# Depthwise convolution of both channel tiles on TensorE: four taps of 32 channels in one contraction, over shifted copies made by on-chip transfers

## The reference, cut to what matters

```python
def conv_module(a, gate, w_dw, b_dw, ln_g, ln_b, w_pw):
    u = a * jax.nn.sigmoid(gate)                     # 272 tokens x 256 channels
    y = lax.conv_general_dilated(u, w_dw[:, None, :], window_strides=(1,),
                                 padding=[(CONV_WIDTH - 1, 0)],      # 31 taps, causal
                                 dimension_numbers=('NWC', 'WIO', 'NWC'),
                                 feature_group_count=D_CONV) + b_dw  # one filter per channel
    y = jax.nn.silu(layer_norm(y, ln_g, ln_b))
    return y @ w_pw
```

## Time and profile before

| | |
|---|---|
| runs of the kernel before, median (lowest to highest of 3) | 1790.46 us (1790.15 to 1790.73) |
| the profiled execution, device time | 1793.75 us |
| its span (first to last instruction) | 1791.9 us |
| PE, DVE, ACT, POOL busy | 96%, 65%, 46%, 13% |
| granted TensorE clock, mean over the span | 0.979 |
| bytes moved | 281.5 MB, mean 157 GB/s |

### The profile page before, as it was taken

The page is one execution under the profiler, slowest core; times in us unless marked ns, Lnnn a source line. Parts: engine busy times, 40 slices in busy tenths (PEclk is TensorE's granted clock), DMA queues, the critical chain, the costliest instruction groups (busy, mean ns, idle before and its releaser), DMA issues.

```text
span 1791.9 us, 32601 instructions
## 1 busy us (share of the span) xinstructions
PE 1713.9 (96%) x13384; PEld 1662.4 (93%) x13384; DVE 1172.3 (65%) x1594; ACT 817.4 (46%) x1062; POOL 237.6 (13%) x212
## 2 busy tenths in 40 slices
PE   7999999999999999999999996999899999889998
PEld 6999999899999999998899995998899998889997
DVE  5556597685566755587686544566866568677664
ACT  5333373563435433364564433564533345354333
POOL 0002400310032000500230042231100020020000
PEclk9999999999999999999999998998999999999998
DMA  5545443344544445442355552332445533144552
GB/s 208 170 181 185 167 150 118 118 165 167 196 172 150 176 172 204 148 174 97 127 194 188 204 194 95 115 133 95 165 177 192 194 141 106 50 143 184 187 204 78
DMA packets 37864, 281.52 MB, mean 157 GB/s; under 512 B 4384, under 2 KB 4512, under 8 KB 7184
## 3 DMA queue, kind: packets, MB, share of 16 engines
q1 hardware_dynamic: 36016, 271.73, 42.3%
q0 software_dynamic: 1760, 8.56, 1.4%
HBM read 279.23 MB, written 1.05 MB: 156 GB/s over the span
## 4 chain that ended last, share of the span: by engine, by line
PE 76%; DVE 10%; ACT 7%; issue 3%; DMA 2%; POOL 1%; SPq 0%; ACTq 0%; DVEq 0%; POOLq 0%
PE bank L682 24%; PE bank L684 23%; PE bank L683 23%; DVE w_lo L2045 4%; ACT w_hi L1422 4%; DMA raw<-in_up_w 1%; ACT h L1486 1%; ACT h_hi L1485 1%; PE bank L1035 1%; POOL h L618 1%; PE bank L1060 0%; PE bank L987 0%; PE bank L703 0%; PE bank L1220 0%; DVE h L2212 0%
## 5 line engine op out<-in xcount | busy, mean ns | idle before, releaser
L2045 DVE TENSOR_TENSOR w_lo<-raw,w_hi 128x2048 fp32r<-128x2048 f32 (+3 forms) x239 | 580.6, 2429 | 277.8 <-ACT w_hi L1422 277.5
L682 PE MATMUL bank<-h_hi,w_hi 128*128 128x272 f32 (+1 forms) x2336 | 673.4, 288 | 21.2 <-DVE h_lo L2201 10.0
L684 PE MATMUL bank<-h_hi,w_lo 128*128 128x272 f32 (+1 forms) x2336 | 669.4, 287 | 0.0
L683 PE MATMUL bank<-h_lo,w_hi 128*128 128x272 f32 (+1 forms) x2336 | 668.1, 286 | 0.0
L1422 ACT ACTIVATE w_hi<-raw 128x2048 fp32r<-128x2048 f32 (+2 forms) x242 | 481.5, 1990 | 316.5 <-PE bank L684 311.7
L682 PEld LDWEIGHTS bank<-h_hi,w_hi 128*128 128x128 f32 x2336 | 444.3, 190 | 27.9 <-issue 16.3
L684 PEld LDWEIGHTS bank<-h_hi,w_lo 128*128 128x128 f32 x2336 | 444.3, 190 | 0.0
L683 PEld LDWEIGHTS bank<-h_lo,w_hi 128*128 128x128 f32 x2336 | 443.5, 190 | 0.1
L682 PE MATMUL bank<-g_hi,w_hi 128*128 128x256 f32 (+1 forms) x1344 | 386.8, 288 | 13.8 <-DVE y L2253 4.0
L684 PE MATMUL bank<-g_hi,w_lo 128*128 128x256 f32 (+1 forms) x1344 | 382.6, 285 | 0.0
L683 PE MATMUL bank<-g_lo,w_hi 128*128 128x256 f32 (+1 forms) x1344 | 381.7, 284 | 0.0
(11 more groups left out here) (363 smaller groups left out, 1863.3 us busy)
## 6 DMA issues: line engine op xcount, KB each, us to landing
raw<-in_up_w SPq DMA_DIRECT2D x131, 1024.0 KB, 4.8
raw<-in_down_w SPq DMA_DIRECT2D x48, 1408.0 KB, 5.9
raw<-in_in_w SPq DMA_DIRECT2D x20, 1024.0 KB, 4.9
raw<-in_out_w SPq DMA_DIRECT2D x16, 1024.0 KB, 4.9
raw<-in_even_w SPq DMA_DIRECT2D x12, 1024.0 KB, 4.9
raw<-in_odd_w SPq DMA_DIRECT2D x6, 1024.0 KB, 4.8
diag<-in_conv_w POOLq DMA_DIRECT2D x4, 1024.0 KB, 5.1
raw<-in_in_w SPq DMA_DIRECT2D x4, 512.0 KB, 3.5
```

The lines of the kernel that those rows point to most:

```text
L682: pe.matmul(out, w[0], x[0], start=first, stop=False)
L683: pe.matmul(out, w[0], x[1], start=False, stop=False)
L684: return pe.matmul(out, w[1], x[0], start=False, stop=last)
L2045: last = dve.tensor_tensor(lo[:, b:n], raw[:, slot, b:n], hi[:, b:n].bitcast(F32), ALU.subtract)
```

## The change

Both channel tiles go to PE. Four taps are put into one contraction: the 128 rows of the stationary operand are 4 taps x 32 channels, its 32 columns are the same 32 channels, and the moving operand holds in its four groups of 32 partitions the same 32 channels shifted by 0, 1, 2 and 3 tokens. So 31 taps are 8 steps (`TAP_STEPS`), and there are 4 groups of 32 channels in each of 2 channel tiles: 64 matmuls with 272 moving columns, each into 32 partitions of bank 4 or 5. The four groups of a step follow one another. The shifted copies `u4` are made from `upad` by 16 transfers, each of 32 partitions x 2 x 300 floats, which SP issues after the load of chunk 6, having waited for `conv_in`. `upad` gets two more zero columns, and `diag`, of the same 1 MB, comes in one transfer. The matmuls all stand after chunk 6 (ahead of the pool mixing). The vector taps go, and the wait for `conv_done` moves ahead of the scores, since these use bank 4 too. ACT adds the bias of both tiles in chunk 7's place.

The diff, less the placing of `u4` in memory and the host's laying out of the gains:

```diff
@@ -40,7 +40,10 @@
 RMS_EPS = 1e-6
 HEADS = 4
 TAPS = 31
-TAP_HALF = 16
+TAP_ROWS = 4
+TAP_STEPS = -(-TAPS // TAP_ROWS)
+TAP_COLS = P // TAP_ROWS
+U4 = T + TAP_ROWS * (TAP_STEPS - 1)
 KTOK = [(0, 128), (128, 128), (256, 16)]
 SEEN_FROM = [max(0, 64 * ((lo - META) // 64) + META) for lo, _ in KTOK]
 SEEN_AT = [0, T, 2 * T - SEEN_FROM[1]]
@@ -52,7 +55,7 @@
 IN_GROUPS = [2] * 10 + [1] * 2
 OUT_CHUNKS = KD // 2
 EVEN_GROUPS = [2] * 12 + [1]
-CONV_AT = (5, 7)
+CONV_AT = 6
 ODD_GROUPS = [2] * 6
 
 
...
@@ -204,12 +207,15 @@
+        u4 = place("u4", [P, 2, TAP_ROWS, U4], offset=u4_at)
-        upad = one("upad", [P, 2, TAPS - 1 + T])
+        upad = one("upad", [P, 2, U4 + TAP_ROWS])
@@ -232,8 +238,8 @@
-        diag = place("diag", [P, TAP_HALF, P], offset=sq_at)
-        few = placer(region((sq_at + TAP_HALF * P * 4, sq_at + KD * T4)))
+        diag = place("diag", [P, 2, TAP_ROWS, TAP_STEPS, TAP_COLS], offset=sq_at)
+        few = placer(region((sq_at + 2 * TAP_STEPS * P * 4, sq_at + KD * T4)))
@@ -373,7 +379,7 @@
         small_done = sem("small_done")
         conv_in = sem("conv_in")
         diag_loaded = sem("diag_loaded")
-        diag_used = sem("diag_used")
+        taps_loaded = sem("taps_loaded")
         conv_mm = sem("conv_mm")
         conv_done = sem("conv_done")
         conv_mean = sem("conv_mean")
@@ -561,14 +567,25 @@
                             load(src[bass.ds(c * 2 + i * n + j, 1)].rearrange("a p n -> (a p) n"), blocks, j, c)
                     st.c += n
 
-            def straight(chunks):
+            def straight(chunks, then=lambda i: None):
                 for i, (src, blocks) in enumerate(chunks):
                     load(src, blocks, i)
+                    then(i)
                 st.c += len(chunks)
+
+            def shifted_taps(l):
+
+
+                sp.wait_ge(conv_in, l + 1)
+                for r in range(TAP_ROWS):
+                    for g in range(TAP_ROWS):
+                        sp.dma_start(u4[TAP_COLS * r:TAP_COLS * (r + 1), :, g, :],
+                                     upad[TAP_COLS * g:TAP_COLS * (g + 1), :, r:r + U4]).then_inc(taps_loaded, 16)
 
             for l in range(LAYERS):
                 ffn(l * 2)
-                straight([(a["in_w"][l, c, :, 0:n * KD * P], n * KD) for c, n in enumerate(IN_GROUPS)])
+                straight([(a["in_w"][l, c, :, 0:n * KD * P], n * KD) for c, n in enumerate(IN_GROUPS)],
+                         lambda c: shifted_taps(l) if c == CONV_AT else None)
                 straight([(a["out_w"][l, c], 2 * KD) for c in range(OUT_CHUNKS)])
                 ffn(l * 2 + 1)
             straight([(a["even_w"][c, :, 0:n * KD * P], n * KD) for c, n in enumerate(EVEN_GROUPS)])
@@ -637,9 +654,7 @@
                     .then_inc(mixw_loaded, 16)
 
                 pool.wait_ge(conv_in, seen.next(conv_in))
-                pool.dma_start(diag[:], a["conv_w"][l, 0]).then_inc(diag_loaded, 16)
-                pool.wait_ge(diag_used, l + 1)
-                pool.dma_start(diag[:], a["conv_w"][l, 1]).then_inc(diag_loaded, 16)
+                pool.dma_start(diag[:], a["conv_w"][l]).then_inc(diag_loaded, 16)
                 if l == LAYERS - 1:
                     first.lo = META
                 residual_sums(2)
@@ -991,18 +1006,18 @@
             for l in range(LAYERS):
                 ffn(T, DEFER if l else 0, l == 0)
 
-                def conv_taps(c):
-
-
-                    for part in range(2):
-                        if c != CONV_AT[part]:
-                            continue
-                        pe.wait_ge(conv_in, l + 1)
-                        pe.wait_ge(diag_loaded, (2 * l + part + 1) * 16)
-                        for i in range(part * TAP_HALF, min((part + 1) * TAP_HALF, TAPS)):
-                            last = pe.matmul(ps[5][:, 0:T], diag[:, i % TAP_HALF, :], upad[:, 1, i:i + T],
-                                             start=i == 0, stop=i == TAPS - 1)
-                        last.then_inc(conv_mm if part else diag_used, 1)
+                def conv_taps():
+
+
+                    pe.wait_ge(diag_loaded, (l + 1) * 16)
+                    pe.wait_ge(taps_loaded, (l + 1) * 16 * TAP_ROWS ** 2)
+                    for j in range(2):
+                        for i in range(TAP_STEPS):
+                            for g in range(TAP_ROWS):
+                                last = pe.matmul(ps[4 + j][TAP_COLS * g:TAP_COLS * (g + 1), 0:T], diag[:, j, g, i, :],
+                                                 u4[:, j, g, TAP_ROWS * i:TAP_ROWS * i + T],
+                                                 start=i == 0, stop=i == TAP_STEPS - 1)
+                        last.then_inc(conv_mm, 1)
 
                 def score(hd):
 
@@ -1065,7 +1080,8 @@
                 def mixers(c):
 
 
-                    conv_taps(c)
+                    if c == CONV_AT:
+                        conv_taps()
                     if c == 6:
                         pe.wait_ge(mixw_loaded, seen.next(mixw_loaded, 16))
                         pe.wait_ge(pool_in, seen.next(pool_in))
@@ -1076,10 +1092,10 @@
                     elif c == 7:
                         pe.wait_ge(rope_ready, seen.next(rope_ready, 2 * HEADS))
                         pe.wait_ge(small_done, seen.next(small_done, 2))
+                        pe.wait_ge(conv_done, seen.next(conv_done, 2))
                         score(0)
                         score(1)
                         score_tails()
-                        pe.wait_ge(conv_done, seen.next(conv_done, 2))
                         for j in range(2):
                             last = pe.matmul(ps[5][:, 0:T], ones[:], conv_y[:, j, :], start=j == 0, stop=j == 1)
                         last.then_inc(conv_mean, 1)
@@ -1766,14 +1782,15 @@
 
 
                     if c == 7:
+                        for j in range(2):
+                            act.wait_ge(conv_mm, seen.next(conv_mm))
+                            act.activation(conv_y[:, j, :], ps[4 + j][:, 0:T], ACT.Identity, bias=vcol(l, V_CDB + j))\
+                                .then_inc(conv_done, 1)
                         act.wait_ge(pool_mixed, seen.next(pool_mixed))
                         for j in range(2):
                             act.activation(y[:, j, :], ps[6 + j][:, 0:T], ACT.Identity, scale=vcol(l, V_PSC + j))\
                                 .then_inc(small_done, 1)
                     elif c == 8:
-                        act.wait_ge(conv_mm, l + 1)
-                        act.activation(conv_y[:, 1, :], ps[5][:, 0:T], ACT.Identity, bias=vcol(l, V_CDB + 1))\
-                            .then_inc(conv_done, 1)
                         for j in range(2):
                             act.wait_ge(conv_cent, seen.next(conv_cent))
                             act.activation(conv_sq[:, j, :], conv_y[:, j, :], ACT.Square).then_inc(conv_sqd, 1)
@@ -2449,6 +2466,7 @@
 
                 ffn(IN_GROUPS[0] * KD, T, l, 0, l > 0)
                 dve.memset(xpad[:, :, 0:16], 0.0)
+                dve.memset(upad[:, :, TAPS - 1 + T:], 0.0)
                 link(dve.memset(upad[:, :, 0:TAPS - 1], 0.0))
 
                 def pool_windows():
@@ -2466,22 +2484,6 @@
                     link(last)
                     dve.tensor_tensor(pool_y[:], pool_y[:], xpad[:, :, 16:W], ALU.subtract).then_inc(pool_in, 1)
 
-                def conv_tap(i):
-
-                    u, w = upad[:, 0, i:i + T], vcol(l, V_DW + i)
-                    out = acc[:] if i % 2 else conv_y[:, 0, :]
-                    if i == 0:
-                        ins = dve.tensor_scalar(out, u, w, vcol(l, V_CDB), ALU.mult, ALU.add)
-                    elif i == 1:
-                        ins = dve.tensor_scalar(out, u, w, None, ALU.mult)
-                    else:
-                        ins = dve.scalar_tensor_tensor(out, u, w, out, ALU.mult, ALU.add)
-                    ins.then_inc(dve_seq, 1)
-                    seen.skip(dve_seq, 1)
-                    dve.wait_ge(dve_seq, seen.at(dve_seq, 0 if i == TAPS - 1 else -1))
-                    if i == TAPS - 1:
-                        dve.tensor_tensor(conv_y[:, 0, :], conv_y[:, 0, :], acc[:], ALU.add).then_inc(conv_done, 1)
-
                 def rope(i):
 
                     dst = (qT if i < HEADS else kT)[:, i % HEADS, :]
@@ -2499,7 +2501,7 @@
                 renormalise(take)
                 take(2)
                 dve.wait_ge(z_copied, seen.at(z_copied, 4))
-                dve.tensor_tensor(upad[:, :, TAPS - 1:], ca[:], cg[:], ALU.mult).then_inc(conv_in, 1)
+                dve.tensor_tensor(upad[:, :, TAPS - 1:TAPS - 1 + T], ca[:], cg[:], ALU.mult).then_inc(conv_in, 1)
                 split_next(2 * KD, 0, 5)
                 dve.wait_ge(conv_in, seen.next(conv_in))
                 seen.skip(q_ready, DEFER)
@@ -2565,8 +2567,7 @@
                     dve.tensor_tensor(y[:, 4 + hd, :], y[:, 4 + hd, :], ps[SCALE_BANKS[hd]][:, 0:T], ALU.mult)\
                         .then_inc(ret_done, 1)
 
```

(23 more changed lines are left out.)

## The result

The changed kernel takes 1800.51 us (median of 7 runs, 1796.03 to 1801.96); the kernel before, run beside it, 1790.73 (7 runs, 1790.15 to 1795.13). The ratio is 1.0040, 95% interval 1.0026 to 1.0054: slower by 4.7 to 9.7 us. The forecast was 3.3 us more with a range of 1790 to 1809: the sign and the range hold, the size was too small, and 3.3 lies outside both intervals.

A forecast was written before the change was run, and what follows sets the result against it. TensorE, busy 96% of the span, was taken to bound the kernel. Per layer -0.83 - 0.33 + 2.1 + 0.7 = +1.6, twice +3.3 us, on 1790.46 gave 1793.8 us, range 1790 to 1809.

The forecast's parts named there:

- the main case: Whole kernel: 3.3 us slower, 1793.8 us, by itself 1791.7 to 1795.8; chance 0.67.
- taps in pairs: Taps after chunk 6: only two column groups run at once, 14.5 us per layer; total +17.8, 1808; chance 0.14.
- taps fed too slowly: Taps after chunk 6: groups overlap but 128 records take 9.9 us; total +8, 1798.5; chance 0.07.
- Term 1a: Before chunk 6: without two vector taps ahead of it, `w_lo` comes earlier, -0.83 us per layer.
- 1b: At the mean matmul: PE's wait on `conv_y` goes, -0.33 us per layer.
- chunk 6 starts before 268.0: Layer 0, PE's start of chunk 6: forecast at 268.07; earlier than 268.0 would show the forecast wrong.
- Term 2: Chunk 6: PE idles 7.5 us before it, so granted clock falls to 0.50 behind; +2.1 us per layer (1.35 to 2.7).
- Term 3: Taps after chunk 6: 64 matmuls four at a time take 7.6 us against 6.88; +0.7 us per layer (0.4 to 1.1).
- Term 4: The 16 shifted copies on SP's queue: issues take 5.3 us, chunk 7's load goes out at about 257; cost 0.
- Term 5: Other edits: ACT's two `conv_y` copies in chunk 7's place, one more DVE memset, order after chunk 7; cost 0.
- everything after chunk 8 as before: Profile after chunk 8: expected unchanged, only 1.6 us later per layer.

The follow-up runs named there:

- the run with fewer vector taps: Kernel before, with 28 of the 31 VectorE taps of channel tile 0 left out, so half of the convolution is not computed: 1789.88 us, ratio 0.9983.
- the version with the taps in the hole and 8 fillers: Changed kernel, its 64 taps moved behind chunk 5 with 8 unused f32 matmuls ahead of them: 1784.08 us, ratio 0.9949 to the kernel before.
- the last filled one: Changed kernel, taps behind chunk 5, six copies issued by ScalarE, 4 and 10 unused matmuls ahead of the taps in layers 0 and 1: 1785.42 us, ratio 0.9960.
- the one with GpSimd: Changed kernel, taps behind chunk 5, eight of the 16 copies issued by GpSimd's queue: 1786.17 us, ratio 0.9965 to the kernel before.

## Why the prediction was right in sign and short in size

By luck the range holds: the main case alone had 1791.7 to 1795.8, and 1800.51 lies within 1790 to 1809 only because this was widened for taps in pairs and for taps fed too slowly, and neither is what happened.

The trace lets each step be read by itself. From the start of chunk 5 to that of chunk 8 layer 0 is 1.31 us longer than before and layer 1 2.24.

- **Term 1a, 1b (-0.83, -0.33): right.** Chunk 6 starts 13.76 us after chunk 5 (253.90 to 267.66) instead of 14.66 (254.24 to 268.90), 0.90 less, and the wait before the mean is gone. The run with fewer vector taps gives 0.88 and 0.40 alone. That chunk 6 starts before 268.0 was named as a sign of being wrong; it starts at 267.66, but this execution was 0.34 us ahead of the one before already at chunk 5.
- **Term 2 (+2.1, 1.35 to 2.7): right in kind, too small.** Chunk 6 lost 1.97 and 2.87 us in the changed kernel's first profile, 2.42 and 2.41 in the second: 2.4 in the mean. I had averaged five stalls of 3 to 4 us; the hole here is 7.4 us, and layer 1 had 6.23 us at 0.50 behind it, longer than any of the five. Whether the longer hole is the reason isn't shown, since behind the same hole layer 0 had 4.23.
- **Term 3 (+0.7): right.** 7.47 us for 6.88, +0.59. Nothing is seen of the 0.1 us at either end. Four column groups reading different data overlap as fully as the narrow tiles of the earlier trace rows; the rivals of pairs (14.5 us) and of weak feeding (9.9) fall. The 9.2 us worked out from the Trainium skill (TensorE: Matmul & The Clock Gate, Measured speedup vs the span model) fall with them: this trace doesn't agree with that share. 29.0 / 7.47 is 3.9 times for four groups of 272 columns in f32.
- **Term 4 (copies, 0): right in the sum, wrong in the working.** I took 0.33 us for an issue from a 1 MB load; a copy takes 0.6 to 1.4, so chunk 7's load went out at 262.05 instead of 257. The slack that I had named held: PE waited for no transfer, and chunk 7 began without a wait (284.06). In the hole, where there is no slack, PE waited 3.4 and 5.1 us for the copies.
- **Term 5 (0): right.** ACT copies the last `conv_y` while it has time to spare, and nothing waits.

The five terms with their measured sizes give -0.90 - 0.33 + 2.4 + 0.59 = +1.8 per layer, 3.5 in all before rounding, where I had 3.3. What is missing is outside the mixers, at the step that said "everything after chunk 8 as before": in the profiled execution the offset to before grows by 1.6 us between chunk 8 of layer 1 (840.81 by 837.62) and 887.17 (by 882.37), which is the stretch of 3.42 us at 0.50 with PE busy, and by 0.67 in a wait on DVE's `y` (1.32 by 0.65) behind it; this wait is 1.31 in the version with the taps in the hole and 8 fillers too, where no such stretch stands ahead of it, so the stretch needn't be its cause. That with the 0.34 us by which this execution began earlier is nearly all of the 5.8 between the spans.

The step that failed is this one: that low clock would come only straight behind the hole, and everything after chunk 8 would be as before. The second profile of the changed kernel, with a span of 1799.4 by 1791.9, shows the same: the stretches from chunk 5 to chunk 8 are 3.5 us longer in both layers together, and a later stretch at 0.50 adds 1.7 us in each layer.

That the hole brings the later stretch too isn't shown. In the 13 profiles, that of the kernel before included, it stands at about the same place in 6 of the 13 layers that have low clock in their mixer ahead of it (3 of 4 in the changed kernel) and in 3 of the 13 that have none: in one layer each of the run with fewer vector taps (321.1 us), of the last filled one (316.8) and of the one with GpSimd (316.6). The runs say that filling the hole takes back all of the loss, some 8 us by ratios that each have an uncertainty of 2 to 3 us. The rows of the second profile come to as much, 4.83 us in chunk 6 and 3.4 in the later stretches; those of the first come to 4.84 and 1.6. How often the later stretch comes stays open.

## What to carry to other kernels

Before work is taken off the engine that sets the time, ask what it stood in: matmuls that fill a wait are free and keep the clock up, and the same matmuls behind the wait are paid in full, with low clock on top. Here the new form of the taps was worth having only in the old place of the taps. In that place it was limited by its transfers: halving their size and doubling their number made it slower, and a second queue shortened the wait in one layer and not in the other. Fewer and larger transfers were not tried. What helped was to cover the rest of the wait with other matmuls.
